# A two-layer transformer block in fp32 halves: a ninth pair of split buffers, splits moved out of the stage boundaries, dummy first products and a reordered attention tail

## The reference

```python
y = rmsnorm(h, g_pre); y = gmlp_mixer(y) ; h = h + rmsnorm(y, g_post)          # 1: stage GMLP
y = rmsnorm(h, g_pre); y = conv_ffn(y)   ; h = h + rmsnorm(y, g_post)          # 2: FFN0
y = rmsnorm(h, g_pre); y = diff_attention(y); h = h + rmsnorm(y, g_post)       # 3: DIFF
y = rmsnorm(h, g_pre); y = conv_ffn(y)   ; h = h + rmsnorm(y, g_post)          # 4: FFN1
h = h + 0.5 * swiglu(rms_norm(h))                                              # 5: FFN2
h = h + (concat(mla_attention, moba_attention)(rms_norm(h))) @ w_out           # 6: MIX
h = h + 0.5 * swiglu(rms_norm(h))                                              # 7: FFN3
out = rms_norm(h)
```

## Time and profile before

| | |
|---|---|
| median of three runs | 1075.33 us |
| the profiled execution's own time | 1076.43 us |
| its span, first to last instruction | 1074.6 us |
| PE busy | 1054.8 us (98%) |
| DVE busy | 776.3 us (72%) |
| ACT busy | 654.5 us (61%) |
| granted TensorE clock over the span | 0.998 of full speed |

### The profile page before, as it was taken

The page is one execution under the profiler, slowest core; times in us unless marked ns, Lnnn a source line. Parts: engine busy times, 40 slices in busy tenths (PEclk is TensorE's granted clock), DMA queues, the critical chain, the costliest instruction groups (busy, mean ns, idle before and its releaser), DMA issues.

```text
span 1074.6 us, 15598 instructions
## 1 busy us (share of the span) xinstructions
PE 1054.8 (98%) x5944; PEld 911.8 (85%) x5944; DVE 776.3 (72%) x1229; ACT 654.5 (61%) x1176; POOL 36.4 (3%) x38
## 2 busy tenths in 40 slices
PE   7999999999999999999999999999999999999997
PEld 5987888888799878888887888888899988888886
DVE  5888988878767889878887755665676857566554
ACT  6767765567657778566667645545556657454454
POOL 0830000000000000000000000000000000000000
PEclk9999999999999999999999999999999999999999
DMA  9763766565463347666554765567345525656651
GB/s 356 229 232 125 252 202 204 186 203 185 171 220 106 111 150 245 194 198 194 183 189 135 239 197 193 177 195 215 129 163 161 197 59 181 211 176 196 190 183 40
DMA packets 56779, 198.14 MB, mean 184 GB/s; under 512 B 6577, under 2 KB 8537, under 8 KB 56705
## 3 DMA queue, kind: packets, MB, share of 16 engines
q1 hardware_dynamic: 56448, 196.94, 56.2%
q0 software_dynamic: 112, 0.20, 0.1%
q10 hardware_dynamic: 144, 0.00, 0.0%
HBM read 195.35 MB, written 1.25 MB: 183 GB/s over the span
## 4 chain that ended last, share of the span: by engine, by line
PE 93%; DVE 4%; ACT 2%; issue 1%; DMA 0%; SPq 0%; ACTq 0%
PE G L1407 27%; PE Y L1465 25%; PE G L1411 14%; PE G L1392 3%; PE G L1393 3%; PE G L1394 3%; PE G L1442 2%; PE G L1443 2%; PE G L1448 2%; PE Y L1460 1%; DVE w_low L855 1%; PE Y L1393 1%; PE Y L1392 1%; PE Y L1394 1%; PE G L1590 1%; PE Y L1473 1%
## 5 line engine op out<-in xcount | busy, mean ns | idle before, releaser
L855 DVE TENSOR_TENSOR w_low<-raw,w_high 128x1024 fp32r<-128x1024 f32 x352 | 425.0, 1225 | 37.4 <-ACT w_high L442 35.7
L442 ACT CAST w_high<-raw 128x1024 fp32r<-128x1024 f32 x352 | 363.8, 1046 | 10.8 <-DMA raw<-in_panels 10.8
L1407 PE MATMUL G<-x_parts,w_high 128*128 128x512 f32 x1280 | 319.6, 392 | 0.0
L1407 PEld LDWEIGHTS G<-x_parts,w_high 128*128 128x128 f32 x1280 | 234.1, 188 | 44.7
L529 ACT COPY big<-G 128x512 f32<-128x512 f32 x80 | 46.8, 585 | 237.9 <-PE G L1411 237.9
L1411 PEld LDWEIGHTS G<-x_parts,w_low 128*128 128x128 f32 x1280 | 174.6, 190 | 12.5
L1411 PE MATMUL G<-x_parts,w_low 128*128 128x256 f32 x1280 | 178.5, 282 | 0.0
L959 DVE TENSOR_TENSOR w<-G,big 128x512 f32<-128x512 f32 x80 | 55.3, 691 | 164.5 <-ACT big L529 164.3
L1465 PE MATMUL Y<-w_high,a_high 128*128 128x512 f32 x420 | 132.0, 395 | 1.1 <-DVE a_low L968 1.1
L1465 PE MATMUL Y<-w_high,a_low 128*128 128x512 f32 x420 | 130.1, 391 | 0.0
L1465 PE MATMUL Y<-w_low,a_high 128*128 128x512 f32 x420 | 129.7, 390 | 0.0
(11 more groups left out here) (246 smaller groups left out, 1185.1 us busy)
## 6 DMA issues: line engine op xcount, KB each, us to landing
raw<-in_panels SPq DMA_DIRECT2D x352, 512.0 KB, 4.3
gain_pre<-in_gains SPq DMA_DIRECT2D x7, 512.0 KB, 6.4
gain_post<-in_gains SPq DMA_DIRECT2D x4, 512.0 KB, 7.0
big<-in_xT SPq DMA_DIRECT2D x4, 256.0 KB, 7.3
h<-in_x SPq DMA_DIRECT2D x2, 512.0 KB, 8.4
big<-rel_rows SPq DMA_DIRECT2D x8, 128.0 KB, 5.0
out_y<-w SPq DMA_DIRECT2D x4, 256.0 KB, 2.2
big<-in_w_s SPq DMA_DIRECT2D x1, 512.0 KB, 10.0
```

Source lines behind the costliest of these rows:

```text
L442: s.copy(WH[:, n % RING, :], raw[:, n % RAWS, :]).then_inc(hi, 1)
L855: v.tensor_tensor(WL[:, n % RING, :], raw[:, n % RAWS, :], WH[:, n % RING, :].bitcast(F32), ALU.subtract).then_inc(lo, 1)
L1407: mm(out, WH[:, n % RING, k * P:(k + 1) * P], X2[:, k, :, :], start=k == 0, stop=False, skip_group_check=True)
```

## The change

Described by part:

- **Ring.** RING is 9 instead of 8. `share` keeps its old leads (8 on ACT, 7 on DVE) up to f = 13 and uses 9 and 8 from f = 14 on. The last `upto` of a feed-forward stage goes one panel further on ACT in all of them, on DVE after the two conv stages; before boundary 3 both engines also take one panel more (DIFF+34).
- **Boundaries.** One `upto(base + 3)`, before `x_normed(b,0)` on DVE and before `h_rms(b,0)` on ACT, takes the place of the two of before. `half_mean` is gone: a column with the value sqrt(EPS * D) stands behind each row of `h` (rows are 1026 long now), the square instruction of the second half takes it in, and both have the scale 1/sqrt(D). `h_add(b,1)` stands before `x_low(b,0,2)`. `first_four` ends in `last_values`, which uses the low parts of x last.
- **End of a conv stage.** `hidden_low` of f = 20 stands between the two pairs of taps of f = 21.
- **Start.** 12 products of `ones` by `ones` (128 x 128, float32) run first, 4 more after the first high part of x. The load of panel 0 is issued by ACT, ahead of `g0`, not by SyncE.
- **Attention of MIX.** `pair_out` of pairs 8 to 10 writes to bank 2 of Y and no longer waits for a copy out of PB; `scores` 9 and 11 move to banks 0 and 1 of Y, and `scores` 9 to 12 wait for the DVE reduction of the pair before; `turn(a,0)` waits for one half of `exps` only. `scores(9)`, `turn(8,1)` and `weigh_values(8,0)` stand between the two tiles of `moba_pair(2)`. For pairs 12 to 14 the output rows of t=0 stand before `weigh_values(a,1)`, then `pair_out(a-1)`, then the rows of t=1; ACT puts `cast(a-1)` between the halves of `exps(a+1)`, and both engines take one panel in every round, the last (base+3 of FFN3) in round 15, ahead of `cast(14)` on ACT and ahead of `outs(15)` and `low_out(14)` on DVE.
- **End.** ACT issues the stores of the first halves itself, SyncE those of the second halves.

The core of the diff:

```diff
-RING = 8
+RING = 9
-        h = sb("h", [P, TT, D])
+        h = sb("h", [P, TT, D + 2])
-            load(0), load(1)
+            load(1)
+            g.memset(h[:, :, D:D + 1], (EPS * D) ** 0.5)
@@ h_rms
-                act.wait_ge(h_sq1, 2 * b + t + 1)
-                act.wait_ge(bt_r, 2 * b + t + 1)
-                s.activation(sd2[:, t:t + 1], ss2[:, t, 1:2], ACT.Sqrt, bias=bt[:, t:t + 1], scale=1.0 / D)\
+                act.wait_ge(h_sq, 4 * b + 2 * t + 2)
+                s.activation(sd2[:, t:t + 1], ss2[:, t, 1:2], ACT.Sqrt, bias=ss2[:, t, 0:1]).then_inc(h_std, 1)
@@ boundary, ACT
                     y_root(b, 0)
-                    upto(base + (3 if b == 1 else 2))
+                    upto(base + 3)
                     h_rms(b, 0)
-                    upto(base + 3)
@@ share, ACT (DVE: 7 and RING - 1)
-                todo = min(seen + RING, PANELS - 1) + 1 - made[0]
+                todo = min(seen + (8 if f < NF - 8 else RING), PANELS - 1) + 1 - made[0]
@@ end of ffn, ACT
-                upto(base + 3 * NF + 1)
+                upto(base + 3 * NF + 2)
@@ boundary, DVE
-                    half_mean(b, 0)
-                    upto(base + (3 if b == 1 else 2))
+                    upto(base + 3)
                     x_normed(b, 0)
                     ...
+                    h_add(b, 1)
                     x_low(b, 0, 2)
-                    h_add(b, 1)
-                    half_mean(b, 1)
-                    upto(base + 3)
@@ end of ffn, DVE
-                upto(base + 3 * NF + 1)
+                upto(base + 3 * NF + (2 if with_conv else 1))
@@ rounds 12 to 15 of MIX, DVE
+                upto(B + 20 + a)
+                outs(a)
                 if a > 12:
                     low_out(a - 1)
-                if a < 14:
-                    upto(B + 20 + a)
-                outs(a)
@@ rounds 12 to 15 of MIX, ACT
                 turned_out(a, 0), turned_out(a, 1)
-                if a > 12:
-                    cast(a - 1)
-                if a < 14:
-                    upto(B + 20 + a)
-                if a < 15:
-                    exps(a + 1)
-                if a >= 14:
-                    upto(B + 34)
+                upto(B + 20 + a)
+                if a == 12:
+                    exps(13)
+                elif a < 15:
+                    exps(a + 1, lambda: cast(a - 1))
+                else:
+                    cast(14)
@@ PE
+            def last_values(b, n, out, t):
+                part = sixth(b, t, 2)
+                ready(n)
+                pe.wait_ge(xh_r, part)
+                ...
+                both(0, WH, 2), both(0, WL, 2)
+                pe.wait_ge(hi, n + 2)
+                both(0, WH, 3)
+                pe.wait_ge(xl_r, part)
+                both(1, WH, 2), both(1, WH, 3)
+                ready(n + 1)
+                return both(0, WL, 3, True)
+            run_up(12)
+            pe.wait_ge(x0h, 1)
+            run_up(4)
             value_panels(0, 0, (0, 1))
```

More of the change, by code:

```diff
@@ L462, in h_rms @@
             def h_rms(b, t):
-                for c, done in ((0, h_sq0), (1, h_sq1)):
+                for c in range(2):
                     if b:
@@ L492, in boundary @@
                 else:
+                    upto(base + 3)
                     h_rms(b, 0)
-                    upto(base + 2)
-                    x_high(b, 0, 0), x_high(b, 0, 1)
-                    upto(base + 3)
-                    x_high(b, 0, 2)
+                    for i in range(3):
+                        x_high(b, 0, i)
                 h_rms(b, 1)
@@ L598, in swiglu_ffn, with exps @@
                     share(f, base, 1)
-            def exps(a):
+            def exps(a, between=None):
                 b = a % 2
@@ L609, in exps @@
                                         accum_out=sm[:, b, 2 + m:3 + m])
+                    if m == 0:
+                        if a >= HEADS:
+                            last.then_inc(ex0_r, 1)
+                        if between is not None:
+                            between()
                 last.then_inc(ex_r, 1)
@@ L1010, in conv_ffn @@
                         hidden_low(ph, f - 1)
-                    if f < NF - 1:
-                        share(f, base, 1)
+                    share(f, base, 1)
                 dve.wait_ge(taps, ph * NF + NF)
@@ L1449, in values, with both @@
                 return last
+            def last_values(b, n, out, t):
+                part = sixth(b, t, 2)
+                ready(n)
+                pe.wait_ge(xh_r, part)
+                def both(level, W_part, q, last=False):
+                    for k2 in range(2):
+                        k = 2 * q + k2
+                        end = mm(out, X2[:, k, level, tok(t)], W_part[:, (n + q - 2) % RING, half(k2)],
+                                 start=False, stop=last and k2 == 1)
+                    return end
+                both(0, WH, 2), both(0, WL, 2)
[5 more added lines that the diff above has]
+                return both(0, WL, 3, True)
             def rows(n, slot, t, first, last):
@@ L1508, in first_four @@
                 n = STARTS[b]
-                for p in range(4):
-                    last = values(b, n + p, p, out[0], 0)
+                for p in range(2):
+                    values(b, n + p, p, out[0], 0)
+                last = last_values(b, n + 2, out[0], 0)
                 if done is not None:
@@ L1609, in _, with run_up @@
             pe.wait_ge(consts, 1)
+            def run_up(n):
+                for _ in range(n):
+                    mm(Y[:, 0, 0:P], ones[:], ones[:], start=True, stop=True)
+            run_up(12)
+            pe.wait_ge(x0h, 1)
+            run_up(4)
             value_panels(0, 0, (0, 1))
@@ L1754, in moba_pair @@
                     tile_out(B + 10 + 2 * j + m, G[:, (j + 1) % 2, m * T:(m + 1) * T])
-                    if j == 1 and m == 0:
-                        column_factors()
+                    if m == 0 and between is not None:
+                        between()
             def mla_q(u):
@@ L1827, in _ @@
             scores(8)
-            moba_pair(1)
+            moba_pair(1, column_factors)
             pe.wait_ge(cb_r, 1)
-            turn(8, 0), scores(9), turn(8, 1), weigh_values(8, 0), moba_pair(2), weigh_values(8, 1)
+            turn(8, 0)
+            moba_pair(2, lambda: (scores(9), turn(8, 1), weigh_values(8, 0)))
+            weigh_values(8, 1)
             turn(9, 0), scores(10), turn(9, 1), weigh_values(9, 0), pair_out(8), moba_pair(3), weigh_values(9, 1)
```

90 lines of the change are left out of this document (44 added, 46 removed).

## The result

The change makes the kernel 0.4% slower: median 1079.98 us (1079.82 to 1081.31, 6 runs) against 1075.47 (1075.19 to 1076.43, 6 runs), ratio 1.0043 [1.0033, 1.0052]. Forecast was 1068.2 us, with 1065.7 to 1071.4 as the range and 0.04 for slower. The profiled execution has a span of 1078.1 us, its own time is 1080.08 and its granted clock 0.998, the same as before. So the profile shows a loss of 3.5 us where it should have shown a gain of 7.1.

What follows compares the result with a forecast made beforehand. The prediction took PE, busy 98% of the span, as the bound, leaving its waits, slow work and the ends to win. Terms of 1.6 + 1.0 + 2 x 0.84 + 0.7 + 0.8 + 0.8 + 0.5 = 7.1 off 1075.33 gave 1068.2 us, range 1065.7 to 1071.4.

Steps and rivals of the forecast that it cites:

- At nothing: Edits costed at zero: leads in `share`, longer rows of `h`, GpSimd memset, new waits of `scores`, the 16 dummies.
- start: Start: dummies raise the clock, first product at 8.1, panel 1 begun at 10.85 instead of 12.45; gain 1.6 us.
- boundary 1: Boundary 1: `x_low(b,0,2)` behind `h_add` and no `half_mean` shorten the chain to the last t=1 piece; gain 1.0 us.
- boundary 2: Boundary 2: PE's wait for the base+3 split goes, the t=0 products start 0.36 us late; gain 0.84 us.
- boundary 3: Boundary 3: PE's idle 1.37 us goes, but a third split delays the t=0 chain; gain 0.7, bounds 0.2 to 1.6.
- boundary 4: Boundary 4: as in boundary 2, the base+3 split wait goes and t=0 starts late; gain 0.84 us.
- boundary 5: Boundary 5: a split leaves the chain before `h_plus_y(b,1)`, t=1 pieces come 1.1 us earlier; gain 0.8 us.
- MIX, boundary 6: MIX and boundary 6: PE waits removed, less a 1.05 us loss at pair 15; gain 0.8, bounds -0.5 to 2.0.
- end: End: two stores issued together save 0.4 us, the root without `half_mean` 0.1; gain 0.5 us, bounds 0.2 to 0.6.
- clock: Rival, start: dummies don't raise the clock, PE idling between them or products too light; 1070.7 us, chance 0.13.
- moved work late: Rival: extra cast and split cost their full 1.2 us in boundaries 2 to 4, round 15 as reckoned; 1070.9, chance 0.15.
- nothing measurable: Rival: removed waits come back as later ones of the same length; within 0.2% of before, about 1074, chance 0.07.

Runs made afterwards that it cites:

- e9: Changed kernel with `h` allocated behind `w3`, so `x_parts` and `a_high` lie a multiple of 4096 bytes from `w_high`; 1072.05 us.
- e1: Kernel before with unused 16-byte tensors behind `h` and `big2`, moving what follows by 16 or 32 bytes; 1083.18 us.
- e6: Changed kernel with unused 96-byte tensors behind `h` and `big2`, and panel 0 loaded by SyncE as before; 1079.45 us.
- e3: Kernel before with the 16 dummy products alone, panel 0 and the gain loaded as before; 1075.02 us.
- e15: Changed kernel with `h` behind `w3`, panel 0 loaded by SyncE, no panel in round 15, and without the 16 dummy products; 1069.81 us (1069.02 with them).
- e2: Kernel before with RING 9 and the old leads in `share`; no difference in time.
- e11: Kernel before with 256 bytes left free behind `h`; time as before, to 0.01%.
- e12: Kernel before with 1024 bytes left free behind `h`; time as before, to 0.01%.
- e4: Changed kernel with unused 48-byte tensors behind `h` and `big2`, putting `x_parts` 96 bytes off; 1086.29 us.
- e13: Kernel before with 32 bytes left free ahead of `w_high`, so all operands lie 32 bytes further; 1075.81 us.
- e14: Kernel before with 32 bytes left free between `w_high` and `w_low` and 224 behind `w_low`; 1079.28 us.
- e5: Changed kernel with unused 96-byte tensors behind `h` and `big2`, so `x_parts` begins at a multiple of 128; 1080.97 us.

## Why the prediction was wrong

The failed step stands under **At nothing**: "the longer rows of `h`", costed at nothing. I priced what they do to the engines that read `h`, even as a rival, and not what they do to the buffers behind `h`. They move `x_parts`, `a_high` and `a_low` by 32 bytes against `w_high` and `w_low`, and so the fp32r products got another pitch (228.6 and 119.1 ns became 233.5 and 117.1): 8.1 us of span (changed kernel 1078.1, e9 1070.0). With it fell the premise under every sum that a product costs 0.229 us before and after. That the place is the cause is shown twice, by e1 (place alone, slower) and by e9 (place alone put back, faster); why the chip does this is not.

The other terms are read at equal placement, e9 against before, one trace of each, as the shift of a mark in the profiled execution (earlier is a gain). Marks: start up to the mixing stage, 52.16 to 52.75; last turn of boundary 1, 92.12 to 91.73; of 2, 279.40 to 278.28; of 3, 392.43 to 390.90; of 4, 579.97 to 577.42; of 5, 766.27 to 762.81; of 6, 890.20 to 885.69; end of the span, 1074.64 to 1070.02. Each gain is the difference of two shifts.

```
term              predicted   measured
start                +1.6       -0.6
boundary 1           +1.0       +1.0
boundary 2           +0.84      +0.7
boundary 3           +0.7       +0.4
boundary 4           +0.84      +1.0
boundary 5           +0.8       +0.9
MIX, boundary 6      +0.8       +1.1
end                  +0.5       +0.1
sum                  +7.1       +4.6
placement             0         -8.1
span                 +7.1       -3.5
```

**Start.** Wrong in sign, in two places. `g0` landed at about 7.6, 1.5 us behind panel 0, where I let it land at once behind, an estimate that no row bore out, and had 0.7 us as the bound: the first product came at 9.51, past my upper bound of 8.8. Behind the panel in ACT's queue the small gain took 6.4 us instead of 4.2, and with the panel moved back to SyncE `g0` takes 4.3 and the first product is at 7.21 (e6). Panel 0 itself landed as I had it: 5.3 us after its issue at 0.74, at 6.0; in 4 to 6 and 6 to 8 us the DMAs moved 340 and 420 GB/s, before 412 and 384. And the last four dummies, which wait for `x0h`, came after 2.2 us in which PE idled. The first twelve had raised the clock near 5.1 us; it fell again near 8.6, 0.4 us after PE resumed, and the first five real products got half clock. In e3, with no pause, and in e6, with one of 0.45 us, it stayed up until the real products. The rival "clock" was half right: PE did idle between the dummies, because of `g0`, but they did raise the clock before, so they are not too light. My other error was to carry the gain of panel 1 whole to the end: e15 shows 2.0 us there and 0.5 at the end. I had seen the limit, the DMA of panel 7, but took it for 2.1 us.

**Boundaries.** Right in sum: it is 4.0 us against 4.2 predicted for 1 to 5. The first turns wait, 0.44 us in boundary 2 and 0.67 in boundary 3 (0.6 and 0.9 forecast), and no split is waited for at t=1. In these two numbers the slower PE hides a part: at equal placement (e9) the waits are 0.90, 0.86 and, in boundary 4, 0.90, so in 2 and 4 the t=0 chain is some 0.3 us later than I reckoned. So the rival "moved work late" wasn't it, nor "nothing measurable". Boundary 3 was optimistic, within its bounds.

**MIX.** The 0.9 us wait at pair 15 is there, 0.83, behind the split as reckoned (forecast: `outs` at 874.0 and `low_out(14)` at 874.4; in the timelines of DVE, then PE, of the changed kernel):

```profile
873.07 1.23 DVE L867 TENSOR_TENSOR w_low<-raw,w_high 128x1024 fp32r<-128x1024 f32 x1 [3.43 <-ACT w_high L448]
874.22 0.85 DVE L1312 TENSOR_SCALAR otk<-G,rs 128x64 f32<-128x64 f32 x4
874.98 0.42 DVE L1320 TENSOR_TENSOR a_low<-G,a_high 128x256 fp32r<-128x256 f32 x1
```

```profile
875.55 0.41 PE L1846 MATMUL G<-cst,otk 128*128 128x128 f32 x2 [0.83 <-DVE a_low L1320]
```

The 0.3 us wait of `scores` 10 for `qk` I had not foreseen.

**End.** The two stores are issued together, as forecast, but the 0.4 us didn't come: from the first issue to the end of the span it was 3.09 us before (1071.55) and is 3.10 now (both lines of the timeline are the changed kernel's). Two stores at once landed later by what the issue had saved: 2.5 us (SyncE's) and 2.7 (ACT's) from issue to landing in the median, 2.2 before.

```profile
1075.00 0.34 SPq L377 DMA_DIRECT2D out_y<-w  x1
1075.03 0.35 ACTq L515 DMA_DIRECT2D out_y<-w  x1
```

The root's 0.1 us is there: last product to first issue 3.34 before, 3.22 now.

In the median the working parts are worth less than in the profile: e9 is 3.5 us below the kernel before, not 4.6. The profiled execution of before was 1.1 us above its median. So the forecast would have missed its range at equal placement too: e9's 1072.05 us is above 1071.4, and the start, which was to give at least 0.5 us, is the term that does it.

## What to carry to other kernels

A change of a buffer's size can move every buffer behind it: 16 bytes more in `h` moved `x_parts`, `a_high` and `a_low` by 32. Before costing the waits, compare the addresses of the operands that TensorE reads; here two columns of padding took back more than all the edits had won, and moving one declaration brought it back. When a saving is made at the very start, follow it to the first wait on a DMA: here, of 2.0 us at panel 1, 0.5 were left at the end, behind the wait for the DMA of panel 7 (e15).

## What the runs showed of the hardware

- The pitch of fp32r matmuls of 512 columns is 228.5 or 228.6 ns where the buffers of held and moving operands lie a multiple of 256 bytes apart in a partition (tried: the distances of before, of e2, e9, e11 and e12), and 231.2 to 233.5 where `x_parts`, `a_high` and `a_low` are 32, 64, 96 or 128 bytes off. That of 256 columns goes from 119.1 to 115.6 at 64 bytes, 117.0 at 32, 119.1 at 128 and 119.6 at 96. The second accounts for the difference between two of the runs: e4 is 6.3 us above the changed kernel, and 2380 times 2.5 ns in the 256 columns are 6.0.
- The distance counts, not the place: moving all of them by 32 bytes changed nothing (e13, the one run that tries it: 228.6 and 119.1 ns, 1075.81 us). Which accesses meet each other isn't shown (e14: 230.7 and 118.3 ns with only `w_low` off).
- A load of 4 KB behind one of 512 KB in the same queue took 6.4 us (6.2 in e5 and e9) instead of 4.2, while SyncE's queue was loading too.
- Of TensorE's clock at the start, by the distance of the dummies' records (0.213 us at the lower level, 0.111 at the upper): busy from 1.06 us, it rose near 5.1 (changed kernel), 4.9 (e6) and 6.1 (e3, busy from 1.03). After 2.2 us idle PE resumed at 8.15 at the upper level, fell to the lower near 8.6, and five real products took 0.427 us each or more (changed kernel; granted clock 0.50 from 8.60 to 11.90). With no pause (e3) or 0.45 us (e6) the real products had the upper level.
